# A conditioned decoder layer on one core: more conditioning work ahead of the first feed-forward unit, the first normalised tile before the samples, and pooled-stage operations issued tile by tile

## The reference, cut to what matters

```python
# x: 256 prompt tokens and 8 sample tokens of width 2048; c: one condition for the prompt, one per sample
sh1,sc1,g1,sh2,sc2,g2 = split(c @ w_ada + b_ada, 6)        # w_ada: 2048 x 12288
u = x * (1 + sc1) + sh1
z, xc, B, C, gate_p, gate_c = split(u @ w_in)              # z, xc, B, C: 1024 wide; gates: 2048
pooled = mean over the last 2, 4, 8, 16 tokens (a group of 256 channels each) of z, minus z
y_p = (per-group linear of pooled * scale) @ w_pool_up
y_c = (B * dwconv3(C * xc)) @ w_conv_up
mixed = (sigmoid(gate_p) * y_p + sigmoid(gate_c) * y_c) @ w_o
x = LN1(ALPHA * x + g1 * mixed)
u2 = x * (1 + sc2) + sh2
x = LN2(ALPHA * x + g2 * (relu(u2 @ w_ff1 + b_ff1)**2 @ w_ff2 + b_ff2))
```

## Time and profile before

| what | value |
|---|---|
| median of 3 runs | 1486.63 us (1486.34 to 1489.24) |
| the profiled execution | 1488.49 us, of which span 1486.6 us |
| TensorE busy | 1460.2 us, 98% |
| VectorE busy | 859.9 us, 58% |
| ScalarE busy | 530.4 us, 36% |
| GpSimd busy | 129.1 us, 9% |
| granted clock | 0.996 |
| memory traffic | 343.37 MB, mean 231 GB/s |

### The profile page before, as it was taken

One profiled execution on the slowest core, in us unless ns is written; L12 is line 12 of the kernel. 1 busy time (PEld: TensorE's weight loads), 2 busy tenths in 40 slices (PEclk: granted clock), 3 DMA queues, 4 the chain that ended last, 5 costly groups with the idle time before them and its releaser, 6 DMA issues.

```text
span 1486.6 us, 28280 instructions
## 1 busy us (share of the span) xinstructions
PE 1460.2 (98%) x11894; PEld 1373.4 (92%) x11894; DVE 859.9 (58%) x1033; ACT 530.4 (36%) x374; POOL 129.1 (9%) x99
## 2 busy tenths in 40 slices
PE   7999999999999999999899999999999999999998
PEld 5888888888988889899699999999999999999997
DVE  2777566565689565547754454554545545455557
ACT  2333223224224323324643433434334333343335
POOL 0000000000280000000040000000000000000970
PEclk9999999999999999999999999999999999999999
DMA  9985888888884986795955555555555555555541
GB/s 317 334 300 208 304 289 312 308 289 306 315 294 169 374 300 244 276 339 170 341 170 170 188 179 178 189 170 183 184 173 187 176 176 191 171 184 183 172 168 59
DMA packets 173854, 343.37 MB, mean 231 GB/s; under 512 B 5890, under 2 KB 15634, under 8 KB 173763
## 3 DMA queue, kind: packets, MB, share of 16 engines
q1 hardware_dynamic: 173022, 341.19, 66.2%
q0 software_dynamic: 368, 1.18, 0.3%
q10 hardware_dynamic: 404, 0.14, 0.0%
HBM read 340.19 MB, written 2.79 MB: 231 GB/s over the span
## 4 chain that ended last, share of the span: by engine, by line
PE 94%; DVE 3%; SPq 1%; DMA 1%; issue 1%; DVEq 0%; ACT 0%; ACTq 0%
PE main L1351 29%; PE main L1352 29%; PE main L1353 29%; PE ps_ada L1382 5%; SPq L349 1%; DMA raw<-in_w_in 1%; DVE w_lo L860 1%; PE ps_adat L1446 1%; DVE PB L1005 0%; DVE G L1220 0%; DVE U L1252 0%; DVE G L1214 0%; DVE PB L1010 0%; DVE G L985 0%; DVEq L1219 0%
## 5 line engine op out<-in xcount | busy, mean ns | idle before, releaser
L860 DVE TENSOR_TENSOR w_lo<-raw,w_hi 128x2048 fp32r<-128x2048 f32 (+1 forms) x213 | 489.8, 2299 | 468.3 <-ACT w_hi L618 467.7
L618 ACT ACTIVATE w_hi<-raw 128x2048 fp32r<-128x2048 f32 (+1 forms) x227 | 429.8, 1893 | 898.3 <-PE main L1353 898.3
L1351 PE MATMUL main<-U,w_hi 128*128 128x264 f32 (+1 forms) x2320 | 662.8, 286 | 10.7 <-issue 3.8
L1353 PE MATMUL main<-U,w_lo 128*128 128x264 f32 (+1 forms) x2320 | 659.2, 284 | 0.0
L1352 PE MATMUL main<-U,w_hi 128*128 128x264 f32 (+1 forms) x2192 | 620.8, 283 | 0.0
L1351 PEld LDWEIGHTS main<-U,w_hi 128*128 128x128 f32 x2320 | 436.7, 188 | 45.2 <-issue 34.5
L1353 PEld LDWEIGHTS main<-U,w_lo 128*128 128x128 f32 x2320 | 436.1, 188 | 0.0
L1352 PEld LDWEIGHTS main<-U,w_hi 128*128 128x128 f32 x2192 | 412.7, 188 | 0.0
L1351 PE MATMUL main<-H,w_hi 128*128 128x264 f32 x1280 | 365.0, 285 | 0.0
L1353 PE MATMUL main<-H,w_lo 128*128 128x264 f32 x1280 | 362.2, 283 | 0.0
L1352 PE MATMUL main<-H,w_hi 128*128 128x264 f32 x1152 | 327.3, 284 | 0.0
(11 more groups left out here) (234 smaller groups left out, 630.6 us busy)
## 6 DMA issues: line engine op xcount, KB each, us to landing
raw<-in_w_ff SPq DMA_DIRECT2D x128, 1024.0 KB, 5.2
ada_raw<-in_w_ada SPq DMA_DIRECT2D x80, 1024.0 KB, 7.0
raw<-in_w_in SPq DMA_DIRECT2D x63, 1024.0 KB, 9.4
raw<-in_w_o SPq DMA_DIRECT2D x16, 1024.0 KB, 9.3
raw<-in_w_pool_up SPq DMA_DIRECT2D x8, 1024.0 KB, 9.7
raw<-in_w_conv_up SPq DMA_DIRECT2D x8, 1024.0 KB, 10.8
PB<-in_w_ada SPq DMA_DIRECT2D x7, 1024.0 KB, 12.8
PB<-in_w_ada SPq DMA_DIRECT2D x8, 512.0 KB, 9.5
```

The lines of the kernel that those rows point to most:

```text
L618: nc.scalar.activation(w_hi[:, s % HL, 0:size], raw[:, s, 0:size], ACT.Copy).then_inc(hi_ready, 1)
L860: tt(w_lo[:, s % HL, 0:size], raw[:, s, 0:size], w_hi[:, s % HL, 0:size].bitcast(F32), ALU.subtract).then_inc(unit_split, 1)
L1351: mm(out, wh, x_hi, start=start, stop=False)
L1353: return mm(out, wl, x_hi, start=False, stop=stop)
```

## The change

Three edits. First, conditioning units 2 to 7 (six instead of four) run ahead of the first feed-forward unit, units 8 to 11 after it, and none after feed-forward unit 1. For that the slot table gets one more stretch (`Uf` tiles 24 to 31); k = 2 and 4 are loaded where 2 and 3 were; k = 3 and 5 wait only for unit 13 of w_o (the last that reads their space) and are issued right after the first feed-forward unit's weights. VectorE waits for the use of k = 3 instead of 2 before it writes u2. Second, tile 0 is normalised before `sample_u2`, and ScalarE's rounding copy of tile 0 waits for the samples through a new semaphore. Third, GpSimd's window additions, the subtraction L526 and the low part L530 are given as one instruction per tile, and the two halves of the product L1005 are one instruction at step 8.

```diff
-GAP_HELD = 4
-GAP_FIRST, GAP_NEXT = 2, (4, 3, 3)
+GAP_EARLY, GAP_MIXED = (2, 4), (3, 5)
+GAP_FIRST, GAP_NEXT = 2, (6, 4)
-        gap_slot = [ada_u[:, 0], ada_u[:, 1], eight_tiles(Uf, 0), eight_tiles(PB, 8),
-                    eight_tiles(PB, 16), eight_tiles(PB, 24), eight_tiles(PB, 0)]
-        gap_slot += [gap_slot[k] for k in (0, 1, 3, 4, 5)]
-        gap_after = {7: 0, 8: 1, 9: 3, 10: 4, 11: 5}
+        gap_slot = [ada_u[:, 0], ada_u[:, 1], eight_tiles(Uf, 0), eight_tiles(Uf, 24),
+                    eight_tiles(PB, 8), eight_tiles(PB, 16), eight_tiles(PB, 24), eight_tiles(PB, 0)]
+        gap_slot += [gap_slot[k] for k in (0, 1, 4, 5)]
+        gap_after = {8: 0, 9: 1, 10: 4, 11: 5}
...
-                elif k < GAP_HELD:
+                elif k in GAP_EARLY:
                     sp.wait_ge(part_done, done(U_WO - 1))
+                elif k in GAP_MIXED:
+                    sp.wait_ge(part_done, done(U_WO + 13))
                 else:
                     sp.wait_ge(part_done, done(U_FF - 1))
...
-            for k in range(GAP_HELD, GAP_ADA - 2):
+            for k in GAP_MIXED:
+                load_gap(k)
+            for k in range(6, GAP_ADA - 2):
                 load_gap(k)
...
-                g_tt(dst[:, first:PT, step:PROMPT], src[:, first:PT, step:PROMPT],
-                     src[:, first:PT, 0:PROMPT - step], ALU.add)
+                for t in range(first, PT):
+                    g_tt(dst[:, t, step:PROMPT], src[:, t, step:PROMPT], src[:, t, 0:PROMPT - step], ALU.add)
...
-            g_tt(A8, A8, z8, ALU.subtract)
+            for t in range(PT):
+                g_tt(A8[:, t, :], A8[:, t, :], z8[:, t, :], ALU.subtract)
...
-            g_tt(U[:, POOL_LO:POOL_LO + PT, :], A8, U[:, POOL_HI:POOL_HI + PT, :].bitcast(F32),
-                 ALU.subtract).then_inc(pooled_ready, 1)
+            for t in range(PT):
+                r = g_tt(U[:, POOL_LO + t, :], A8[:, t, :], U[:, POOL_HI + t, :].bitcast(F32), ALU.subtract)
+            r.then_inc(pooled_ready, 1)
...
+                if t == 0:
+                    act.wait_ge(u2_samples, 1)
                 nc.scalar.copy(U[:, t, :], Uf[:, KC + t, :]).then_inc(u2_hi_ready, 1)
...
-                if at in (8, 9):
-                    half = slice((at - 8) * PT // 2, (at - 7) * PT // 2)
+                if at == 8:
                     dve.drain()
-                    tt(v[:, half, :], v[:, half, :], y[:, half, :], ALU.mult)
+                    tt(v, v, y, ALU.mult)
...
-            dve.wait_ge(ada_used, gap_used(2))
-            sample_u2()
+            dve.wait_ge(ada_used, gap_used(3))
             for t in range(KC):
...
                 normalise(t, 1, prompt).then_inc(ln_norm, 1)
+                if t == 0:
+                    sample_u2()
...
-            ff1_block(0, 0, gap={1: (at, GAP_NEXT[1]), 2: (at + GAP_NEXT[1], GAP_NEXT[2])})
+            ff1_block(0, 0, gap={1: (at, GAP_NEXT[1])})
```

More of the change, by code:

```diff
@@ L242, in build_layer @@
             sem("pooled_ready"), sem("yp_ready"), sem("yc_ready"), sem("mixed_ready"))
+        u2_samples = sem("u2_samples")
         avg_ready, ln_in, ln_mean, ln_d, ln_sq, ln_sums, ln_moment, ln_var, ln_std, ln_norm = (
@@ L446, in _ @@
             load_wo(1)
-            for k in range(2, GAP_HELD):
+            for k in GAP_EARLY:
                 load_gap(k)
@@ L1246, in sample_u2 @@
                 dve.drain()
-                tt(s, s, sh, ALU.add)
+                tt(s, s, sh, ALU.add).then_inc(u2_samples, 1)
             def lo_u2(c, t, n):
```

## The result

The changed kernel takes 1491.59 us (median of 12 runs, 1490.21 to 1492.76), the kernel before 1488.47 in the same series (12 runs, 1486.34 to 1489.56): ratio 1.0022, 95% interval 1.0013 to 1.0031, 3.1 us slower where 2.1 us less were forecast. The profiled execution took 1490.91 us, with a span of 1488.8.

The account below looks back on a forecast made before the run. TensorE holds 94% of the chain, so only its waits, 6.8 us together, could be won. Gains of 1.8 (pooled), 0.3 (conditioning units) and 0 (first tile) gave 1486.63 - 2.1 = 1484.5 us; own range 1483.6 to 1486.0, 8 in 10 1482.2 to 1488.1.

Parts of the forecast that it names:

- the eight multiplications: Pooled stage, step 9: the eight L1010 on VectorE pass beside GpSimd's tiles without waiting, taking 2.23 us.
- the landings of conditioning units 10 and 11: At the norm: their transfers land at 724.2 and 726.9, so feed-forward unit 1 starts at about 728.0, 1.8 later.
- Tiles and product: Pooled stage: GpSimd tiles take 0.60 and 0.73 us, the whole product 2.36, and the 1.20 idle before unit 58 goes.
- rival A: Pooled stage: VectorE's short instructions, L1010 too, alternate with GpSimd's tiles; 5.8 us on L1010, 1.7 lost, 1488.0 total; chance 0.14.
- the gain of 2.5: Pooled stage: TensorE's idle of 1.20 before unit 58 and 1.31 before unit 59 both disappear.
- The 0.7 that I put on units 60 and 61: Pooled stage: VectorE's eight L1017 stand behind remaining low-part tiles; TensorE sees about 0.7 us as small waits there.
- landings at 697.4 + 2.5 + 2.70 n: At the norm: transfers start 2.5 us after the issue at 697.40, then one MB lands every 2.70 us.
- The bound that I gave: At the norm, the low case: k11, conditioning unit 11's transfer, lands a further 0.9 late, making the gain -0.6 us.
- the 0.3 of gain: At the norm, conditioning units run ahead: feed-forward unit 3 starts at 740.5 instead of 740.85.
- waited 0.66 for u2, as computed: At the norm: TensorE waits 0.5 to 0.7 us for VectorE's L1252 before feed-forward unit 3.
- First tile: At the norm: tile 0 before the samples brings its low part 0.4 us earlier, but gains 0 while transfers hold TensorE.
- units 2 to 7 without a wait: At the norm: these conditioning units run from 709.31 to 714.9, their transfers in on time.

Follow-up runs that it names:

- e12: e3 with the eight multiplications of 264 elements made one of 2112 (part of the computation changed): that instruction took 1.30 us; one profile 1489.76 us.
- e3: The changed kernel with GpSimd waiting for the end of unit 60 before its low part: 1488.15 us, ratio 0.9998 to the kernel before.
- e1: The kernel before with the pooled edit alone (GpSimd tiles, undivided product): 1488.36 us, ratio 1.0001 to the kernel before.
- e6: The changed kernel with conditioning units 10 and 11 computed after feed-forward unit 1, loads unchanged: 1487.90 us, ratio 0.9997 to the kernel before.
- e4: The changed kernel with the loads of conditioning units 10 and 11 issued before the next feed-forward weights: 1487.85 us, ratio 0.9996 to the kernel before.
- e10: The changed kernel with the sample operations ahead of the first tile again, without ScalarE's wait: 1491.44 us, ratio 1.0030 to the kernel before.
- e2: The changed kernel without its pooled edit, so the norm edits alone: 1490.71 us, ratio 1.0015 to the kernel before.
- e7: The kernel before with GpSimd's undivided low part held until unit 60 is done, nothing else changed: 1487.41 us, ratio 0.9995 to the kernel before.
- e8: The changed kernel with low part held and loads of units 10 and 11 first, all GpSimd operations undivided: 1487.52 us, ratio 0.9990 to the kernel before.
- e11: The changed kernel with low part held, loads of units 10 and 11 first, only the low part tiled: 1483.78 us, ratio 0.9975 to the kernel before.

## Why the prediction was wrong

It failed in two steps: the eight multiplications, taken to pass beside GpSimd, and the landings of conditioning units 10 and 11, put too early. The fall of the clock had no term at all. Two smaller terms were off as well, and are named below.

**Tiles and product: right.** Between VectorE's turns a window tile took 0.575 us (409.22, four in 2.30) and a tile of L532 0.71 ((7.08 - 4.94) / 3, from the two lines below, which are the tiles that run in 428 to 432 and in 428 to 430), against 0.60 and 0.73. The product came at 2.51 against 2.36, and the 1.20 before unit 58 is gone.
```profile
425.47 7.08 POOL L532 TENSOR_TENSOR Uf<-Uf,PB 128x264 f32<-128x264 f32 x7
```
```profile
425.47 4.94 POOL L532 TENSOR_TENSOR Uf<-Uf,PB 128x264 f32<-128x264 f32 x4
```

**The eight multiplications: wrong, and the step that decided the pooled stage.** I wrote of L1010 that it "does not run at the double rate and has one SBUF input, like L1045, so I let it pass beside GpSimd". The rate was misread. 2.23 us over 8 x 264 elements is 1.06 ns each with the fixed part of eight short instructions in it, set against 0.60 of one long cast; the old trace had the comparison that was due. These are its lines of the second half of L1005 and of one L1045 alone:
```profile
433.76 0.43 DVE L1045 TENSOR_TENSOR G<-main,G 128x264 f32<-128x264 f32 x1 [0.75 <-PE main L1353]
...
443.63 1.26 DVE L1005 TENSOR_TENSOR PB<-PB 128x1056 f32<-128x1056 f32 x1
```
L1005 (1056 elements, 1.26) and L1023 (2112, 2.36) make the plain rate 1.04 ns and 0.16 fixed, 0.43 for 264 elements, which is what L1045 takes alone, and one L1010 took 0.36 (444.98). In a row L1010 took 0.28 apiece (2.23 / 8) where L1045 took 0.37 (1.10 / 3). e12 measures the rate: 1.30 for 2112 elements, the double rate. That the instructions of 264 elements run in the same way is inferred, from these two differences and from what they do beside GpSimd.

The eight take 2.21 to 2.23 us with GpSimd idle (before, e3), and 5.28 beside six tiles of L537 (the first two are through at 440.06, the last ends at 444.61). L1053, which reads one operand from PSUM, passed at 0.36 apiece just ahead of them (438.65, four in 1.44), beside the same tiles. This is rival A's mechanism at its place, with a smaller price: it asked for eight tiles and 5.8 us, and 3.1 were lost to six. Set on the start of the windows (2.0 earlier), unit 59 started at 450.1, 0.1 later than before, where A had 451.6. So the stall took back the gain of 2.5 and 0.1 more. The 0.7 that I put on units 60 and 61 did not come: no tile was left beside the multiply-adds (3.24 from 448.94, as before), and no idle stands there.

The Trainium skill has it, "VectorE: DVE Perf Modes", section "Mode 2×_2P", and "SBUF — State Buffer", section "Who interferes with whom": such an instruction streams one tensor through both read ports, and while GpSimd holds the port pair that the two share, it waits. Both halves agree with these runs, the rate with 1.30 us in e12 and the contention with 5.28 against 2.21. I had cited the rule and set it aside for a rate wrongly worked out.

**The clock: not in the working at all.** No step priced a fall of the granted clock behind a stall. In the profile of after it is 1.5 on unit 59, of which 1.2 reach the end of the pooled stage (89.13 against 87.90 in e1); it came in three of six profiles with this stall.

**The landings of units 10 and 11: wrong, and the step that decided the norm.** The rate was right. From unit 7 to unit 11 five MB take 728.10 - 714.60 = 13.50 us, 2.70 each, as forecast. But "landings at 697.4 + 2.5 + 2.70 n" puts unit 7 at 712.75 when it is set on after's first issue (696.75), and it started at 714.60, 1.85 later. Between 697.00 and there 17.6 us at 348 GB/s moved 6.1 MB, while the five transfers up to unit 7's are 5.24: by this count 0.9 MB belonged to transfers behind it in the queue. It was not that the queue ran dry before units 6 and 7 were issued: 2.5 MB had moved by 705 of the 3.1 that were issued earlier. Nor is the lateness fixed. In e6, with the same loads, unit 7 started 17.04 us after the first issue instead of 17.85, with 5.9 MB moved (344 GB/s); the forecast was 16.0. The bound that I gave, "if k11 lands a further 0.9 late, -0.6", was half of what came.

Unit 11, too, started 1.85 later than forecast once both are set on the issue that starts the queue (697.40, now 696.75), and the 0.3 of gain less 1.85 is the 1.6 lost. e4 and e6, which take the wait for units 10 and 11 off feed-forward unit 1 or shorten it, each give it back. Unit 3 of feed-forward waited 0.66 for u2, as computed.

**First tile: right in size** (e10: nothing), and TensorE is held by a transfer, as I said, but already by unit 7's. I had units 2 to 7 without a wait and the first feed-forward unit at 715.3; unit 7 waited 1.65 us, and the unit started at 715.60, with everything around it 0.65 earlier.

**The sum.** +1.35 and +1.6 make 2.95 in the profiles, 3.1 in the medians. The forecast of 1484.5 stood on the 1486.63 of three runs, and twelve runs of the same kernel gave 1488.47: of the 7.1 between forecast and measurement 1.8 are that base, 2.1 the gain that did not come, and 3.1 the loss.

How much of the loss is the clock can be estimated from the runs: the share of the clock not granted, times the span, is 9.6 us in the mean over the 12 runs of after (clock 0.9936) and 7.9 over the 33 runs of the kernel before that stood beside e1 to e4 (0.9947). That is 1.7 of the 3.0 between their mean times, 1491.46 and 1488.42, an estimate that takes in every place where the clock fell. The parts in e1 and e2 make 0.1 + 1.5 = 1.6 parts in a thousand against 2.2 of both together; the intervals allow it, and what is left of the difference stays open.

Near the end of the span the clock falls in every profile, in after earlier (0.57 in 1480 to 1482, before 0.94): SP's last issue comes 1485.45 - 1479.72 = 5.7 us after the one that opens the stores of the result, where it was 1482.70 - 1478.77 = 3.9. The span of this profile is 2.2 longer, which is 2.95 less the 2.0 of the beginning and 1.3 more at the end. What moves that fall was not tried; that the two stretches alone come so near the medians' 3.1 is in part chance. A had a chance of 0.14, and its 1488.0 still missed what happened, since it took the landings as forecast.

## What to carry to other kernels

Whether a VectorE instruction passes beside GpSimd is read from a row where the two do overlap; where it has to be inferred from a rate, two sizes of the same form are needed, to part the fixed time from the rate. A block of GpSimd work is best put where VectorE has slack and in tiles: moved alone it stalled the next short line, tiled alone it met the next dense group. Units that wait for transfers go behind work that is ready, and a landing time is computed from the bytes of all that share the queue, not only from those ahead: here that difference was 1.0 to 1.9 us.

## What the hardware showed that I had not expected

Behind a stall of TensorE of 1.2 to 2.7 us the granted clock went to 0.50 (448 to 454 in after, 470 to 474 in e7, 722 to 730 in e3, 714 to 717 in e1) or stayed at 1.00 behind the same stall in another execution. Where it fell it cost 1.2 (pooled stage of after) to 1.9 us (the norm of e3) beyond the stall. In e1 it cost nothing: the slower first feed-forward unit only used up the wait for u2 behind it, 0.33 us instead of 1.75, and the norm is 41.30 against 41.61 before. Which of the stalls it follows changed from profile to profile, and it could fall behind two of them in one execution (e8: 134 to 138 and 470 to 476). What chooses was not settled.

One GpSimd instruction of 2112 elements (4.77 us) held a VectorE instruction of 64 elements for 4.00 us (e7); beside eight tiles that line takes 0.70 instead of 0.23, and GpSimd 9.93 (e11).
